# Dense gates: one 16-bit compare writes the right one-hots of 12 tokens, ScalarE weights 4 of them and one GpSimd multiply weights 8

## What is computed

```python
q = (xb @ wq).reshape(TOK_BLOCK, PEER_HEADS, 2, PEER_HALF)
s = einsum('thcd,hcnd->thcn', q, sub_keys)
top_s, top_i = lax.top_k(s, PEER_TOPK)              # 16 of 128 keys, for each of the 2 halves
cand_s = top_s[:, :, 0, :, None] + top_s[:, :, 1, None, :]
cand_i = top_i[:, :, 0, :, None] * 128 + top_i[:, :, 1, None, :]
fs, fi = lax.top_k(cand_s.reshape(...), PEER_TOPK)  # 16 of 256 pairs
idx = take_along_axis(cand_i, fi)
g = softmax(fs)
a = gelu(einsum('td,thkd->thk', xb, u[idx]))
y = einsum('thk,thkd->td', g * a, v[idx])
```

## Time and profile before

| | |
|---|---|
| three runs, median | 4044.55 us (4040.15 to 4044.76) |
| span of the profiled execution | 4043.5 us (the profile gives no other time of its own) |
| TensorE busy | 3793.5 us (94%) |
| VectorE busy | 3269.8 us (81%) |
| ScalarE busy | 1769.0 us (44%) |
| GpSimd busy | 988.0 us (24%) |
| gate loop, first compare to last matmul, layer 0 / 1 | 112.8 / 112.9 us |

### The profile page before, as it was taken

One profiled execution on the slowest core, in us unless ns is written; L12 is line 12 of the kernel. 1 busy time (PEld: TensorE's weight loads), 2 busy tenths in 40 slices (PEclk: granted clock), 3 DMA queues, 4 the chain that ended last, 5 costly groups with the idle time before them and its releaser, 6 DMA issues. The chain is left out here.

```text
span 4043.5 us, 55694 instructions
## 1 busy us (share of the span) xinstructions
PE 3793.5 (94%) x20589; PEld 3188.6 (79%) x20589; DVE 3269.8 (81%) x6832; ACT 1769.0 (44%) x2928; POOL 988.0 (24%) x796
## 2 busy tenths in 40 slices
PE   6999999978999999999989898897789999999999
PEld 3555789677999999999854646896779999999998
DVE  2755648987999999999863525389979999999998
ACT  2324622185444444444423545322854444444443
POOL 0000000074333333333200000000743333333332
PEclk8999989999999999999989999898999999999999
DMA  6320020269999999999741010200799999999997
GB/s 238 136 94 11 22 89 37 98 174 361 420 419 414 405 403 404 404 404 406 312 177 43 1 42 1 109 37 22 185 375 420 417 412 407 405 405 405 405 406 300
DMA packets 268125, 1033.69 MB, mean 256 GB/s; under 512 B 147056, under 2 KB 150064, under 8 KB 159920
## 3 DMA queue, kind: packets, MB, share of 16 engines
q0 software_dynamic: 77184, 562.07, 34.7%
q1 hardware_dynamic: 190672, 468.07, 30.4%
HBM read 970.69 MB, written 59.39 MB: 255 GB/s over the span
## 5 line engine op out<-in xcount | busy, mean ns | idle before, releaser
L1637 POOL DMA_INDIRECT gbuf<-in_uv,rows x340 | 514.5, 1513 | 866.3 <-DVE hT L1821 796.5
L1429 POOL TENSOR_SCALAR pqT<-iota,selT 128x128 f32<-128x128 f32 x256 | 203.4, 809 | 1337.4 <-ACT selT L1371 1300.9
L1821 DVE SCALAR_TENSOR_TENSOR hT<-gbuf,act,hT 128x1024 f32<-128x1024 f32 x336 | 416.9, 1282 | 6.0
L1806 DVE SCALAR_TENSOR_TENSOR gbuf<-gbuf,ht 128x1024 f32<-128x1024 f32 x340 | 402.3, 1220 | 10.7 <-DMA gbuf<-in_uv,rows 10.7
L1637 POOL DMA_INDIRECT xT<-in_uv,rows x172 | 256.9, 1493 | 471.0 <-DVE hT L1821 392.9
L1653 PE MATMUL ps<-h1h,U1h 128*128 128x384 f32 x1024 | 344.5, 336 | 7.7 <-DVE U1l L1780 7.6
L1653 PE MATMUL ps<-h0h,U0h 128*128 128x384 f32 x1024 | 344.7, 337 | 5.1 <-DVE U0l L1780 5.1
L1653 PE MATMUL ps<-h0h,U0l 128*128 128x384 f32 x1024 | 344.2, 336 | 0.0
L1653 PE MATMUL ps<-h0l,U0h 128*128 128x384 f32 x1024 | 343.9, 336 | 0.0
L1653 PE MATMUL ps<-h1h,U1l 128*128 128x384 f32 x1024 | 343.9, 336 | 0.0
L1653 PE MATMUL ps<-h1l,U1h 128*128 128x384 f32 x1024 | 343.5, 335 | 0.0
(11 more groups left out here) (379 smaller groups left out, 9053.6 us busy)
## 6 DMA issues: line engine op xcount, KB each, us to landing
ring<-in_u SPq DMA_DIRECT2D x128, 1024.0 KB, 13.4
ring<-in_v SPq DMA_DIRECT2D x128, 1024.0 KB, 9.4
ring<-in_wts SPq DMA_DIRECT2D x26, 2048.0 KB, 8.3
gates<-ring SPq DMA_DIRECT2D x32, 1536.0 KB, 8.5
ring<-gates SPq DMA_DIRECT2D x64, 768.0 KB, 16.4
abuf<-in_ada_mid POOLq DMA_DIRECT2D x16, 1024.0 KB, 5.1
xT<-in_ada_late SPq DMA_DIRECT2D x16, 1024.0 KB, 4.8
abuf_c<-in_ada_late POOLq DMA_DIRECT2D x8, 1024.0 KB, 5.1
```

The costliest lines, as they stand in the source:

```text
L1429: last = pool.tensor_scalar(one2[:, r % 2, t, :], iota[:], selT[:, 1, t0 + t:t0 + t + 1], selT[:, 2, t0 + t:t0 + t + 1], ALU.is_equal, ALU ...
L1637: pool.indirect_dma_start(out=slots[m % GSLOTS], out_offset=None, in_=inp[f"uv{l}"], in_offset=bass.IndirectOffsetOnAxis(ap=rows[:, c:c + ...
L1806: v.scalar_tensor_tensor(u, u, 1.0, ht[:, m // P, :], ALU.mult, ALU.mult, accum_out=act4[:, n % 2, m % 2:m % 2 + 1]).then_inc(sem(n_ + "do ...
L1821: v.scalar_tensor_tensor(y, x, w, y, ALU.mult, ALU.add).then_inc(sem(n_ + "acc"), 1)
```

## The change

VectorE now writes all 12 right one-hots of a step unweighted, by one compare, into a new view `hot` of the tile `eq`, in 16-bit floats. Its inputs are 16-bit too and both lie in SBUF: `sel16`, a 16-bit copy of the pick columns, and `iota16`. ScalarE makes these copies ahead of the loop. ScalarE weights the first 4 tokens, from `hot` to `one2`, and GpSimd the other 8, by one multiply. Both wait for the compare (`gm_eq`). The two tensor_scalar of VectorE and the four of GpSimd are gone.

```diff
-        SUB, DIRECT, SCALED = 12, 2, 6
+        SUB, SCALED = 12, 4
+        hot = eq[:].rearrange("p a h s k -> p (a h s k)")[:, 0:2 * SUB * P].rearrange("p (b t n) -> p b t n", b=2, t=SUB)
...
                     act.wait_ge(sem(n_ + "t"), tb + 1)
+                    act.copy(sel16[:, tb * P:(tb + 1) * P], ps[:, 5, P:2 * P])
...
-                    for t in range(DIRECT, DIRECT + SCALED):
-                        at = act.activation(one2[:, r % 2, t, :], one2[:, r % 2, t, :], ACT.Identity,
+                    for t in range(SCALED):
+                        at = act.activation(one2[:, r % 2, t, :], hot[:, r % 2, t, :], ACT.Identity,
...
+                act.copy(iota16[:], iota[:])
...
-                    t0 = r * SUB
-                    pool.wait_ge(sem(n_ + "selT"), (t0 + SUB - 1) // P + 1)
-                    if r >= 2:
-                        pool.wait_ge(sem("gm_mm"), r - 1)
-                    for t in range(DIRECT + SCALED, SUB):
-                        last = pool.tensor_scalar(one2[:, r % 2, t, :], iota[:], selT[:, 1, t0 + t:t0 + t + 1],
-                                                  selT[:, 2, t0 + t:t0 + t + 1], ALU.is_equal, ALU.mult)
-                    last.then_inc(sem("gm_pool"), 1)
+                    t0 = r * SUB + SCALED
+                    pool.wait_ge(sem("gm_eq"), r + 1)
+                    pool.tensor_tensor(one2[:, r % 2, SCALED:SUB], hot[:, r % 2, SCALED:SUB],
+                                       selT[:, 2, t0:t0 + SUB - SCALED].unsqueeze(2).to_broadcast([P, SUB - SCALED, P]), ALU.mult)\
+                        .then_inc(sem("gm_pool"), 1)
...
-                    n = SCALED
-                    v.tensor_tensor(one2[:, r % 2, DIRECT:DIRECT + n],
-                                    selT[:, 1, t0 + DIRECT:t0 + DIRECT + n].unsqueeze(2).to_broadcast([P, n, P]),
-                                    iota_ps.unsqueeze(1).to_broadcast([P, n, P]), ALU.is_equal).then_inc(sem("gm_eq"), 1)
-                    for t in range(DIRECT):
-                        v.tensor_scalar(one2[:, r % 2, t, :], iota_ps, selT[:, 1, t0 + t:t0 + t + 1],
-                                        selT[:, 2, t0 + t:t0 + t + 1], ALU.is_equal, ALU.mult)
+                    v.tensor_tensor(hot[:, r % 2], sel16[:, t0:t0 + SUB].unsqueeze(2).to_broadcast([P, SUB, P]),
+                                    iota16[:].unsqueeze(1).to_broadcast([P, SUB, P]), ALU.is_equal).then_inc(sem("gm_eq"), 1)
```

More of the change, by code:

```diff
@@ L1210, in expert_choice @@
     def expert_choice(l, w3, pqT, keysT, selT, rows, gates, steps, sc, s2, cand, c2, vals, idxu, posu, idxp, ranks, posh,
-                      shift, fs, first, eq, tabs, sel, mrow):
+                      shift, fs, first, eq, tabs, sel, mrow, sel16, iota16):
         n_ = "ch_"
@@ L1872, in expert_layer @@
                               sb(s2, f"first{l}", [P, 2, 16, 16], F16), sb(s2, f"eq{l}", [P, 2, HP, 16, 16], F16),
-                              sb(s2, f"tabs{l}", [P, 2, HP, 16, 16], F16), sb(s2, f"sel{l}", [P, TB, 2, HP, 16]), sb(s2, f"mrow{l}", [2, 2, 256]))
+                              sb(s2, f"tabs{l}", [P, 2, HP, 16, 16], F16), sb(s2, f"sel{l}", [P, TB, 2, HP, 16]), sb(s2, f"mrow{l}", [2, 2, 256]),
+                              sb(s2, f"selT16{l}", [P, TD], F16),
+                              sb(s2, f"iota16{l}", [P, P], F16))
             def pair(name, shape):
```

## The result

The changed kernel takes 4058.53 us (median of 5 runs, 4057.42 to 4060.36), the kernel before 4044.55 (4040.15 to 4048.65). The ratio is 1.0037, with a 95% interval of 1.0024 to 1.0049: slower by 14 us. The forecast of 4080 had the sign right, and the profile shows its mechanism, but its +36 is 2.5 times what came: it had put GpSimd's multiply at 2.40 us, and that took 1.90.

A forecast was written before the change was run, and what follows sets the result against it. All four engines stood within 0.3 us of the gate loop's period. Compare and multiply alternating at 4.05 us a step, plus the ends, gave +18.3 us in layer 0 and +17.7 in layer 1, +36.0: 4080 us, range 4034 to 4108.

The forecast's parts named there:

- The compare at one column per beat, 1.75 us: VectorE's new 1536-column 16-bit compare in the gate loop runs at single rate, 1.75 us, not 0.95.
- Exclusion: In each gate-loop step, VectorE's compare and GpSimd's multiply block each other: 1.75 + 0.05 + 2.40, less 0.15, 4.05 us.
- The multiply, 2.40 us: GpSimd's new two-input multiply of 1024 columns in each gate-loop step takes 2.4 us.
- The store wait at the end, -2.9 and -3.4: At the gate loop's end, ScalarE's wait for a gate store goes: -2.87 us in layer 0, -3.4 in layer 1.
- The first matmul, +0.67: At the gate loop's start, first compare to first matmul takes 4.30 us instead of 3.63: +0.67 a layer.
- The lookups, -0.6 a layer: Ahead of the gate loop, GpSimd no longer runs beside the table lookups: about -0.6 us a layer.
- ScalarE's casts at no cost: ScalarE's four new 128-column casts ahead of the loop, 0.25 us each, lie hidden behind VectorE's own chain.
- TensorE's clock at 1.00: TensorE's granted clock in the gate loop stays 1.0 after the first steps, though busy only 72% of a step.
- (1): Rival: hardly any exclusion; single-rate compare and left one-hots fill VectorE at 3.33 us a step: 4045 us; chance 0.08.
- (2): Rival: the compare runs at double rate, 0.95 us, so the gate loop's period is 3.25: 4037 us; chance 0.14.
- (4): Rival: GpSimd's multiply much dearer than 2.4: 4126 us at 3.2, 4306 at 6.3; low TensorE clock 4164; chance 0.13.
- The case that I named as making the forecast wrong: If GpSimd's multiply proves below 1.7 us, VectorE's left one-hots hide it and the gate loop's period falls to 3.4.

The follow-up runs named there:

- ten tokens: Changed kernel, but ScalarE weights 2 tokens of a step and GpSimd's one multiply 10 (1280 columns): 4079.36 us, 1.0085 of the kernel before.
- with the wait left in place: Changed kernel, with the compare's iota read from PSUM in 32 bits; the compare still waits for the matmuls of step r - 2: 4052.87 us.
- with it moved: Changed kernel with iota from PSUM, and the compare waiting for scalings and multiply of step r - 2, no longer the matmuls: 4040.81 us.

## Why the prediction was wrong in its size, and what of it held

The step that failed is the price of GpSimd's multiply: put at 2.40 us, measured 1.90. With it the step of the loop was put at 4.05 us and came to 3.58. The order of work and the exclusion that turn this price into a loss were right.

- **The compare at one column per beat, 1.75 us.** Right, and the walk is shown to be its cause.
- **Exclusion.** Right in kind: shown by one input from PSUM (no stretch) and by ten tokens (0.68 in place of 0.25). The overlap at the multiply's end, for which the rows left 0 to 0.5 and I took 0.15, was measured as 0.15 and 0.14; that the choice fell so near was luck. The hand-over was 0.09, not 0.05. The row it was read from, GpSimd's tensor_scalar held up by L1463, is of an instruction that at 1024 columns did not hold back a compare begun later: the right conclusion from a row that carries only half of it.
- **The multiply, 2.40 us.** This is the term that failed. It took 1.90. I had scaled VectorE's two-input instruction by the ratio of the two engines on tensor_scalar, 1.97. That ratio belongs to another kind of instruction, which on GpSimd costs 0.36 us fixed, against the multiply's 0.18, and twice the price per column. With the measured 1.90 the forecast's formula gives a step of 3.55, measured 3.58. The 58 intervals came out 27.1 us below the forecast (103.86 and 103.92 against 117.45 each), which takes +36.0 to +8.9. The store waits at the end give 3.2 back, the start and the last step take 2.2, and the lookups 0.2: +9.6 in the two stages, as measured.
- **The store wait at the end, -2.9 and -3.4.** It shrank by 1.4 and 1.7 only, since at 3.58 a step the stores are 7.2 us apart and not 8.1. With ten tokens, where they are 8.0 apart, the last copy did end 1.5 us after TensorE.
- **The first matmul, +0.67.** +0.35 (3.98 against 3.63), with the shorter multiply. The forecast let this delay reach step 2. It did not: in layer 0 step 2 starts 8.89 us after the first compare, where it had been 9.23. From the first matmul to the compare of step 2 it took 4.91 us (827.45 to 832.36), at a granted clock of 0.60 on the mean, in place of 5.60 at 0.50.
- **The lookups, -0.6 a layer.** -0.75 in layer 0 and -0.7 in layer 1; L1463 and L1466 are back at the 2.29 and 2.41 us of the earlier trace rows.
- **ScalarE's casts at no cost, TensorE's clock at 1.00.** Both held; the stretch 840 to 940 was granted 1.00 with TensorE busy 81%.
- **The rivals.** (1) was the price of the change without exclusion: 4045 forecast, 4052.9 measured with the wait left in place and 4040.8 with it moved. It left out the two-step loop. (2) gave 4037 at double rate, with a multiply of 2.40; 4034.4 measured, with 1.90. (4), a dearer multiply and a fall of TensorE's clock, did not come with the change; with GpSimd's tensor_scalar of 3.78 us in the multiply's place both came, and 4151.87 us. The case that I named as making the forecast wrong, a multiply hidden by the left one-hots, was near: at 1.90 most of it is hidden, and the step is 0.25 above VectorE's own.

## What to carry to other kernels

Before an instruction is split over VectorE and GpSimd, add up compare + hand-over + multiply as a cycle of its own wherever both have two SBUF inputs. And add up the double-buffered chain through all engines, halved: at 3.59 and 3.44 us these two stood above every engine's own work of 3.33. Do not price an engine's instruction by the ratio of another kind; take two sizes of the same kind, or keep the range as wide as the two rows leave it. A 16-bit compare against a value repeated along the innermost dimension is no faster than a 32-bit one.

## What the runs showed of the hardware

- GpSimd, two-input multiply with one 16-bit input: 0.18 us + 1.67 ns a column. tensor_scalar with two operations: 0.36 us + 3.3 ns a column; with one, 2.84 us for 1024 columns. The instruction with more tensor inputs is the cheaper one.
- A GpSimd two-input multiply holds back a VectorE instruction with two SBUF inputs until 0.15 us before its recorded end (2.00 and 2.43 us in place of 1.75). A tensor_scalar of GpSimd on 1024 columns that was under way did not (1.76 in 3.78 and in 2.84), while one that started during such a VectorE instruction waited for it (2.45 us in place of 0.79), and the 128-column ones cost such VectorE instructions 0.13 and 0.40 us. That second tensor inputs and the scalars of each partition (pick and gate) share a way which a first tensor input does not use would fit all of these; it was not tested.
- TensorE's granted clock from 840 to 940 (1.00 is 2.4 GHz, 0.50 is the low level of 1.2): with gaps of 1.1 us in a step of 4.0 it was 1.00 (the ten-token run), and with gaps of 1.6 and 0.4 us in turn too (the tensor_scalar of 2.84 us). With a gap of 3.2 us after every two groups (the tensor_scalar of 3.78 us) the mean was 0.83, between the two levels:

```profile
840.00:940.00 100.00, 72.43 (x598) 68.40 (x598) 100.00 (x51) 53.20 (x75) 57.66 (x26) 1.00 0.75 197
```

```profile
840.00:940.00 100.00, 70.44 (x471) 69.01 (x472) 63.92 (x39) 50.53 (x95) 72.36 (x20) 0.83 0.60 158
```

The first row is of the ten-token run and the second of the tensor_scalar run of 3.78 us, by stretch as in the earlier trace rows. TensorE is busy 72% and 70% of them, and the busy time of the second is itself lengthened by the low clock.
